# HGRN2 layers' score steps by four blocks, the keys' decay on GpSimd, and two joins between layers reordered

## What is computed

```python
b = jnp.cumsum(lc, axis=-2)                      # lc: log of the forget gate
diff = b[..., :, None, :] - b[..., None, :, :]
decay = jnp.exp(jnp.where(causal[:, :, None], diff, NEG_BIG))
scores = jnp.einsum('bhtk,bhsk,bhtsk->bhts', qc, kc, decay)
o = scores @ vc + jnp.einsum('bhtk,bhkv->bhtv', qc * jnp.exp(b), state)
```

## Time and profile before

| | us |
|---|---|
| median of 3 runs (1487.65 to 1491.38) | 1487.92 |
| the profiled execution | 1488.65 |
| its span | 1486.9 |
| TensorE, matmuls busy | 1444.3 |
| VectorE busy | 960.8 |
| ScalarE busy | 663.6 |
| GpSimd busy | 6.5 |

### The profile page before, as it was taken

How to read it: one execution, slowest core, us unless ns; L and a number is a source line. 1 busy time by engine, 2 the same in 40 slices (tenths; PEclk the granted TensorE clock), 3 DMA queues, 4 the chain that set the end, 5 groups by cost and what they waited for, 6 DMA issues and landing times.

```text
span 1486.9 us, 24212 instructions
## 1 busy us (share of the span) xinstructions
PE 1444.3 (97%) x9165; PEld 1296.3 (87%) x9165; DVE 960.8 (65%) x1755; ACT 663.6 (45%) x1174; POOL 6.5 (0%) x16
## 2 busy tenths in 40 slices
PE   6999999889999999999999998999998999999989
PEld 6888888789998989898999996899887988888878
DVE  6677677654475757575757568567656666776772
ACT  6343333442455555555555646455333424333340
POOL 1000000000000000000000000000000000000000
PEclk9999999999999999999999999999999999999999
DMA  6322212143222222231313131423324222221111
GB/s 197 86 57 78 64 56 62 52 121 94 78 72 71 75 69 85 59 88 55 99 44 100 43 100 29 118 61 94 88 83 113 72 59 85 57 85 56 56 57 57
DMA packets 211721, 114.26 MB, mean 77 GB/s; under 512 B 3742, under 2 KB 209744, under 8 KB 211632
## 3 DMA queue, kind: packets, MB, share of 16 engines
q1 hardware_dynamic: 211200, 112.54, 26.3%
q0 software_dynamic: 432, 0.47, 0.1%
HBM read 110.90 MB, written 2.10 MB: 76 GB/s over the span
## 4 chain that ended last, share of the span: by engine, by line
PE 90%; DVE 5%; issue 3%; ACT 2%; DMA 0%; ACTq 0%; DVEq 0%; SPq 0%
PE ps L545 37%; PE ps L533 35%; PE ps L667 5%; PE ps L813 2%; PE ps L830 2%; PE ps L799 2%; DVE w_lo L1441 1%; PE ps L779 1%; PE ps L696 1%; PE ps L559 1%; PE ps L698 1%; PE ps L685 1%; PE ps L842 0%; DVE op_lo L1480 0%; DMA xt<-in_x 0%
## 5 line engine op out<-in xcount | busy, mean ns | idle before, releaser
L545 PE MATMUL ps<-w_hi,op_hi 128*128 128x256 f32 (+2 forms) x1280 | 418.6, 327 | 17.5 <-DVE op_lo L1485 10.3
L545 PE MATMUL ps<-w_lo,op_hi 128*128 128x256 f32 (+2 forms) x1280 | 404.6, 316 | 0.0
L545 PE MATMUL ps<-w_hi,op_lo 128*128 128x256 f32 (+2 forms) x1280 | 404.4, 316 | 0.0
L533 PE MATMUL ps<-op_hi,w_hi 128*128 128x512 f32 (+1 forms) x800 | 321.6, 402 | 2.2 <-DVE op_lo L1480 2.2
L533 PE MATMUL ps<-op_lo,w_hi 128*128 128x512 f32 (+1 forms) x800 | 307.0, 384 | 0.0
L533 PE MATMUL ps<-op_hi,w_lo 128*128 128x512 f32 (+1 forms) x800 | 305.9, 382 | 0.0
L1441 DVE TENSOR_TENSOR w_lo<-raw,w_hi 128x1024 fp32r<-128x1024 f32 x200 | 242.7, 1226 | 96.2 <-ACT w_hi L1010 96.1
L545 PEld LDWEIGHTS ps<-w_hi,op_hi 128*128 128x128 f32 x1280 | 244.4, 191 | 34.3 <-DVE op_lo L1485 13.2
L545 PEld LDWEIGHTS ps<-w_lo,op_hi 128*128 128x128 f32 x1280 | 244.1, 191 | 5.8
L545 PEld LDWEIGHTS ps<-w_hi,op_lo 128*128 128x128 f32 x1280 | 244.7, 191 | 4.8 <-issue 0.2
L1010 ACT ACTIVATE w_hi<-raw 128x1024 fp32r<-128x1024 f32 x200 | 205.0, 1056 | 43.4 <-PE ps L545 30.5
(11 more groups left out here) (174 smaller groups left out, 1591.2 us busy)
## 6 DMA issues: line engine op xcount, KB each, us to landing
raw<-in_b_w_in SPq DMA_DIRECT2D x80, 512.0 KB, 3.8
raw<-in_a_w_in SPq DMA_DIRECT2D x64, 512.0 KB, 4.2
raw<-in_c_w_in SPq DMA_DIRECT2D x24, 512.0 KB, 4.5
raw<-in_a_w_out SPq DMA_DIRECT2D x16, 512.0 KB, 4.0
raw<-in_b_w_out SPq DMA_DIRECT2D x8, 512.0 KB, 4.0
raw<-in_c_w_out SPq DMA_DIRECT2D x8, 512.0 KB, 4.9
xt<-in_x SPq DMA_DIRECT2D x4, 512.0 KB, 8.2
y<-in_norm_w SPq DMA_DIRECT2D x4, 512.0 KB, 4.6
```

Source lines behind the costliest of these rows:

```text
L533: last = nc.tensor.matmul(bank, a, b, start=(k == 0 and p == 0), stop=(k == KT - 1 and p == 2))
L545: last = nc.tensor.matmul(bank, a, b, start=(k == 0 and p == 0), stop=(k == KT - 1 and p == 2))
```

## The change

Levels are taken two at a time. For m = 2, 8, 32, each group of four blocks is handled by one matmul per tile of 192 columns: 96 queries (blocks 1, 2, 3) moved to the border of the block before, and the same from a second plane `a_far`, where they are moved on by one block (blocks 2, 3) and two (block 3). VectorE makes the second plane (`far_queries`, `farthest_queries`) and copies the three distances out with three masks (`keep_quad`). Level 1 stays the ones-matmul. PSUM banks 2 and 3 become one tensor. The keys' multiplies go to GpSimd, which had no work in the layers. TensorE's steps stand at other `ks`. In VectorE's body `split_products` stands behind `carry`, and the last head's weight splits 4 to 6 at the end. At B's entry the pieces are ordered by halves of the features, and TensorE takes the first four steps of two token tiles before their last four. At C's exit `wide` takes all four tiles in one step, and the weight splits go behind all `split_y`.

The diff at its core (twelve columns of indentation and empty lines taken off; masks, the `h_lo` side of the new order, semaphores and counts left out):

```diff
@@ -40,10 +40,15 @@
 WIDE = 4
 NARROW = ((0, 0), (0, 1), (1, 0), (1, 1), (0, 2), (1, 2), (0, 3), (1, 3))
 OUT_UNITS = WIDE + len(NARROW)
+B_ENTRY = tuple((t, 0) for t in range(4)) + tuple((t, 1) for t in (3, 0, 1, 2))
 FINAL = tuple(WIDE + 1 + NARROW.index((1, t)) for t in range(4))
 C_V_CHUNKS, C_UG_CHUNKS = 8, 16
 LEVELS = 7
-G_STEPS = LEVELS + 1
+QUADS = (2, 8, 32)
+G_STEPS = 2 + len(QUADS)
+KEPT = 2 + 3 * len(QUADS)
+QUAD_MASK = 3 * P // 4 + P // 2 + P // 4
+MASKS = P + P // 2 + QUAD_MASK * len(QUADS)
...
+        def move_keys(n):
+            m = 1 << n
+            nb = S // (2 * m)
+            start = 2 * S - 2 * S // m
+            decay = a_t[:, prev, start:start + 2 * nb].rearrange("p (b u) -> p b u", u=2)[:, :, 1]
+            k = a_k[:, prev].rearrange("p (b u m) -> p b u m", u=2, m=m)[:, :, 0, :]
+            if n:
+                pool.wait_ge(keys_moved, h * LEVELS + n)
+            nc.gpsimd.tensor_tensor(k, k, decay.unsqueeze(2).to_broadcast([P, nb, m]),
+                                    ALU.mult).then_inc(keys_moved, 1)
+        if mix:
+            pool.wait_ge(qk_done, h + 1)
+            move_keys(0)
+            for r in range(len(QUADS)):
+                pool.wait_ge(g_ready, h * G_STEPS + 3 + r)
+                move_keys(2 * r + 1)
+                move_keys(2 * r + 2)
...
+            m = QUADS[r]
+            pe.wait_ge(far_done, h * 6 + 2 * r + 2)
+            pe.wait_ge(keys_moved, h * LEVELS + 2 * r + 1)
+            pe.wait_ge(sd_done, h * KEPT + 2 + 3 * r)
+            for t in range(TT):
+                tile = slice(t * P, (t + 1) * P)
+                of = a_qq[:, prev, :, tile].rearrange("p x (h c) -> p x h c", c=4 * m)[:, :, :, m:]
+                last = nc.tensor.matmul(scores2[:, t * 256:t * 256 + 192], a_k[:, prev, tile], of,
+                                        start=True, stop=True)
+            last.then_inc(g_ready, 1)
         def turn_k():
-            pe.wait_ge(upd, h * LEVELS + LEVELS)
+            pe.wait_ge(keys_moved, h * LEVELS + LEVELS)
             if later:
...
@@ -720,16 +766,19 @@
         steps = {}
         if mix:
-            steps[1] = [turn_v]
-            for g in range(G_STEPS):
-                steps.setdefault(int(2 + 2.4 * g), []).append(lambda g=g: scores(g))
-            steps[21] = [turn_k]
-            steps[23] = [states]
+            for g in range(2):
+                steps[g] = [lambda g=g: scores(g)]
+            steps[1].append(turn_v)
+            steps[4] = [lambda: quad_scores(0)]
+            for r, at in ((1, 10), (2, 16)):
+                steps[at] = [lambda r=r: quad_scores(r)]
+            steps[20] = [turn_k]
+            steps[22] = [states]
             steps[27] = [values]
         if end:
-            steps.setdefault(3, []).append(turn_o)
+            steps.setdefault(4 if mix else 3, []).insert(0, turn_o)
         if mix and not proj:
...
-        for ks in range(B_BANKS * KT):
+        order = list(range(B_BANKS * KT))
+        if static(i) and i == 0:
+            order[4:12] = order[8:12] + order[4:8]
+        for ks in order:
             v, k = divmod(ks, KT)
             if proj:
                 bank = acc[v % 2]
+                if static(i) and i == 0 and ks in (0, 8, 4):
+                    pe.wait_ge(h_lo, 8 * n + {0: 4, 8: 5, 4: 8}[ks])
                 if k == 0:
                     if v in (0, 4, 8, 12, 13):
                         upto = {0: 2, 4: 5, 8: 8, 12: 9, 13: 10}[v]
@@ -986,9 +1040,7 @@
     for g in range(5, HEADS):
         spatial(g)
     for k in range(KT - 1):
-        wide(n, k, (0, 1))
-    for k in range(KT - 1):
-        wide(n, k, (2, 3))
+        wide(n, k, range(TT))
 for t in range(2):
     transpose_x(0, t)
...
+        for t, half in B_ENTRY:
+            h_hi_part(n, t, half)
+def h_hi_part(n, t, half):
+    act.wait_ge(xT_done, 8 * n + 2 * t + half + 1)
+    nc.scalar.activation(h_part(op_hi, n, t, half), turned_part(n, t, half),
+                         ACT.Copy).then_inc(h_hi, 1)
 def h_hi_parts(n, t):
...
@@ -1410,11 +1467,9 @@
         if g >= 1:
             act.wait_ge(cgate_done, g)
         nc.scalar.activation(c_g[:, 0], acc[1][:], ACT.Sigmoid).then_inc(cg_act, 1)
-    for k in range(4):
+    for k in range(KT - 1):
         split_y(n, k)
     split_out(n, (4, 5, 6))
-    for k in range(4, KT - 1):
-        split_y(n, k)
 act.wait_ge(s_set, 1)
...
-            h_lo_parts(n + 1, t)
+    if n + 1 < layers and early:
+        h_lo_parts(n + 1, TT - 1)
+    elif n + 1 < layers:
+        for at, (t, half) in enumerate(B_ENTRY):
+            h_lo_part(n + 1, t, half, at)
...
-                                                score[0][:])
-            else:
-                m = 1 << (g - 1)
-                to = a_sd.rearrange("p t (b u m) -> p (t b) u m", u=2, m=m)[:, :, 1, :]
-                mask = a_mask[:, S + (g - 1) * 256:S + g * 256].rearrange("p (b m) -> p b m", m=m)
-                of = score[g % 2][:, 0:256].rearrange("p (b m) -> p b m", m=m)
-                ins = nc.vector.copy_predicated(to, mask, of)
-            ins.then_inc(sd_done, 1)
+            nc.vector.tensor_tensor(q, q, decay.unsqueeze(2).to_broadcast([P, nb, m]),
+                                    ALU.mult).then_inc(queries_moved, 1)
...
+            dve.wait_ge(sd_done, h * KEPT + count)
+        def far_queries(r):
+            m = QUADS[r]
+            nb = S // (4 * m)
+            start = 2 * S - 2 * S // m
+            decay = a_t[:, prev, start:start + 4 * nb].rearrange("p (b u) -> p b u", u=4)
+            q = a_q[:, prev].rearrange("p (b u m) -> p b u m", u=4, m=m)
+            far = a_far[:, prev].rearrange("p (b u m) -> p b u m", u=4, m=m)
+            moved(2 * r + 1)
+            nc.vector.tensor_tensor(far[:, :, 2:4], q[:, :, 2:4],
+                                    decay[:, :, 1:3].unsqueeze(3).to_broadcast([P, nb, 2, m]),
+                                    ALU.mult).then_inc(far_done, 1)
+        def farthest_queries(r):
+            m = QUADS[r]
+            nb = S // (4 * m)
+            start = 2 * S - 2 * S // m
+            decay = a_t[:, prev, start:start + 4 * nb].rearrange("p (b u) -> p b u", u=4)
+            far = a_far[:, prev].rearrange("p (b u m) -> p b u m", u=4, m=m)
+            dve.wait_ge(far_done, h * 6 + 2 * r + 1)
+            nc.vector.tensor_tensor(far[:, :, 1], far[:, :, 3],
+                                    decay[:, :, 1].unsqueeze(2).to_broadcast([P, nb, m]),
+                                    ALU.mult).then_inc(far_done, 1)
+        def keep_own():
+            mask = a_mask[:, 0:P].unsqueeze(1).to_broadcast([P, TT, P])
+            nc.vector.copy_predicated(a_sd, mask, score[0].rearrange("p (t c) -> p t c", t=TT)).then_inc(sd_done, 1)
+        def keep_pairs():
+            to = a_sd.rearrange("p t (b u) -> p t b u", u=2)[:, :, :, 1]
+            mask = a_mask[:, P:P + 64].unsqueeze(1).to_broadcast([P, TT, 64])
+            nc.vector.copy_predicated(to, mask, score[1][:, 0:256].rearrange("p (t b) -> p t b", t=TT)).then_inc(sd_done, 1)
+        def keep_quad(r, back):
+            m = QUADS[r]
+            nb = P // (4 * m)
+            to = a_sd.rearrange("p t (b c) -> p t b c", c=4 * m)[:, :, :, back * m:]
+            of = scores2[:].rearrange("p (t c) -> p t c", c=256)[:, :, 0:192]
+            of = of.rearrange("p t (x b c) -> p t x b c", x=2, b=nb)
+            of = (of[:, :, 0], of[:, :, 1, :, m:], of[:, :, 1, :, 0:m])[back - 1]
+            at = P + 64 + QUAD_MASK * r + (0, 96, 160)[back - 1]
+            wide = 4 * m - back * m
+            mask = a_mask[:, at:at + nb * wide].rearrange("p (b c) -> p b c", b=nb)
+            nc.vector.copy_predicated(to, mask.unsqueeze(1).to_broadcast([P, TT, nb, wide]),
+                                      of).then_inc(sd_done, 1)
         def carry():
...
             if mix:
-                taken(g)
-                gate() if g == 0 else move_on(g)
-                keep(g)
-            if mix and not proj and g > 1:
-                split_y(n, g - 2)
-            if g == 0 and end:
-                into_y()
-            if mix and not proj and g in (1, 2):
-                split_lo_out(n, g + 1)
-            if mix and not proj and g in (5, 6, 7):
-                split_lo_out(n, g - 1)
-            if proj and g in (1, 2):
-                split_lo_chunk(IN0[n], len(A_PARTS), j, par, g + 1, a_ring)
-            if g == 3 and proj:
-                forget()
-            if g == 6 and proj:
-                query()
-            if g == 7 and proj:
-                products()
-            if g >= 4 and proj:
-                decays({4: (0,), 5: (1, 2), 6: (3, 4), 7: (5, 6)}[g])
-        if mix and not proj:
-            split_y(n, 6)
+                taken(2 + r)
+                kept(2 + 3 * r)
+                move_queries(2 * r + 1)
+                keep_quad(r, 1)
+                moved(2 * r + 2)
+                kept(3 + 3 * r)
+                move_queries(2 * r + 2)
+                keep_quad(r, 2)
```

(31 more changed lines are left out.)

## The result

The changed kernel takes 1466.9 us (median of 4 runs, 1466.3 to 1467.8) where the kernel before takes 1489.3 in the same series: a ratio of 0.985 (95% interval 0.983 to 0.987). The forecast was 1464.5. (The 1487.92 that the forecast started from was the median of the first three of the four runs before.) The profiled execution took 1467.06 us, its span 1465.3, 21.6 less than before.

A forecast was written before the change was run, and what follows sets the result against it. TensorE, busy 97% of the span, was taken as the bound. 19.7 + 1.1 + 1.2 + 4.25 - 3 = 23.3 us off 1488.65 gave 1465.4, or 1464.6 against the median; forecast 1464.5, range 1453 to 1470.

The forecast's parts named there:

- Price of a group: TensorE's score groups: three of 192 columns at 1.37 us replace six at 0.89, saving 19.7 us over 16 heads.
- the term of 1.1 us for one return less in 14 heads: TensorE, turn_o directly before the first group: one 0.08 us return to the projection saved per head, 1.1 us.
- Rival D: TensorE's score passes: holes in the streamed operand halve its rate, 61 us lost, 1526 us; chance 0.03.
- The waits: Steady heads: GpSimd's keys' multiplies disturb VectorE's, 0.2 us in each of 14 heads, 3 us lost; ends 0 and 34.
- the chain's slack: VectorE between two groups: chain of 2.9 us inside a 3.8 us cover, 0.9 spare; cover about 0.4 at the first group.
- Rival B: Disturbance with 0.8 to 1.0 us multiplies, or 0.9 us copies: 0.6 to 1.2 us per head lost, 1470 to 1483; chance 0.20.
- A's band: Whole kernel as forecast, 1453 to 1470 us; chance 0.60.
- Rival C: Exclusion with 1.2 us GpSimd multiplies: TensorE waits before groups 1 and 2, 1500 us; loss from about 1.05; chance 0.09.
- The drains: Last head of each HGRN2 layer: idle stays about 5 us and the clock still falls, gain 0, bounds -2 to +2.
- Attention entry: Attention layer's start: TensorE starts 2.4 us earlier, half kept because of the lower clock, 1.2 us; bounds 0 and 4.2.
- gMLP exit: gMLP layer's output steps: three TensorE gaps of 1.32, 1.47 and 1.46 us vanish, 4.25 us saved; bound below 3.
- The prediction's own signs: Trace checks: 192-column passes starting at 0.16 us, heads about 30.3 us; wrong if passes exceed 0.2 or heads aren't below 31.

The follow-up runs named there:

- 96-column run: Changed kernel with the weight split ahead of into_y, each score pass streaming 96 columns (one plane) instead of 192; 1436.1 us, single execution.
- flat operand: Changed kernel with each score pass streaming 192 side-by-side columns of one plane instead of runs with holes; 1467.1 us, single execution.
- the kernels without waits: Changed kernel with GpSimd on one element (1452.0 us), second and third groups one step later (1454.7), weight split ahead of into_y (1453.9), or the last two together (1454.1).
- the better order: Changed kernel with VectorE's weight split of chunk 2 ahead of into_y instead of behind it; 1453.9 us (ratio 0.976).

## Why the prediction was right, and where its terms were off

The sum was 23.3 us against the profiled execution; 21.6 came. The parts:

- **Price of a group.** Forecast 1.37, measured 1.31 without a wait, 1.40 with one (1.26 + 0.14). Three groups are 4.11 in the changed kernel, as forecast. The forecast took 8 x 0.161 for the stream and 0.08 more for the return. But 1.31 is 8 x 0.163: the stream is right, and there is no return beside it. In the trace the passes of a group start 0.163 apart, the projection matmul only 0.03 behind the last of them, and its slower start makes up for that. In the same way a 64-column group costs 0.90 = 8 x 0.112, and the term of 1.1 us for one return less in 14 heads stood for nothing: turn_o's four transposes take 0.43 up to the group now (107.44 to 107.87) and took 0.35 with 0.09 of return before. The floor under the 64-column passes is shown by the 96-column run; that it is the weight load was argued only. Nor is it shown that streaming sets the 128-column passes: the 14 of the values step cost (1.48 + 0.31 - 0.23) / 14 = 0.111 each, the same as 64 and 96 columns. Rival D is excluded by the flat operand.
- **The waits.** The term that was mis-sized. 3 us were taken for 14 heads, 0.2 each; twelve heads wait and lose 0.8 to 1.0 each, 11.4 us (the kernels without waits are 13 us faster in all). Two things were missed. The text set the chain against the cover for one group at a time, and took VectorE to be ready for the second. But all of VectorE's work between two groups has to fit: behind the first it is 5.5 us (chain, weight split, forget, first gate product), and TensorE's interval is 5.4. So lateness of 0.5 at the first group is carried to the next one instead of ending. That uses up part of the chain's slack (0.9 by the prediction), and the 0.56 of exclusion is then more than what is left. And exclusion reached an instruction outside the chain, the gate product L1638 (mean 750 ns against 426 in the better order). Rival B had the mechanism and a size of 0.6 to 1.2 a head, which is what the steady heads show; the total stayed in A's band because the groups and the ends of the layers gave more than forecast (below), which was luck. The exclusion itself is as the Trainium skill tells it in "SBUF — State Buffer", section "Who interferes with whom": this trace agrees, the engine that starts second takes 0.98 or 0.81 instead of 0.42, and in the better order it is VectorE that starts first at the first group and takes 0.43. The estimate of 0.56 us plus dispatch per multiply (from "GPSIMD Engine Reference") meets 0.71 where two take 1.42 (0.65 and 0.69 with a pause between them), and 0.83 as the mean.
- **Rival C.** Its turning point of 1.05 us wasn't reached; mean 0.83.
- **The drains.** Forecast 0, measured 2.2 and 2.7 for the last heads, of which 1.2 was counted for the groups' price. The idle times came as laid out, 1.54 and 3.98 (forecast 1.5 and 3.5):

```profile
260.69 1.54 PE L713 MATMUL scores<-scratch 128*128 128x192 f32 x8 [1.54 <-DVE scratch L1718]
266.21 2.74 PE L713 MATMUL scores<-scratch 128*128 128x192 f32 x8 [3.98 <-DVE scratch L1707]
```
  What was wrong is the clock. In this row of stretches the granted clock is the third number from the end (0.87):

```profile
262.00:275.00 13.00, 9.02 (x37) 7.61 (x36) 11.67 (x23) 5.82 (x9) 4.49 (x6) 0.87 0.29 82
```
  13 x 0.13 = 1.7 us of clock are given up, where the earlier trace rows had 3.4. The lower level lasted half as long, though the idle time ahead of it was longer. In part this is the luck of the execution: over 264 to 282 the granted clock is 0.91 in the changed kernel and in the runs with the flat operand and with the old gMLP exit, and 0.81 in the run with the old attention entry, though the code up to there is the same or, with the flat operand, takes as long. The last heads of the four take 28.60, 28.34, 28.34 and 29.67, and in the second HGRN2 layer 28.36, 29.28, 28.45 and 29.12. So about 1 us of a last head's gain comes and goes with the clock. What decides it, no run here tells.
- **Attention entry.** Forecast 1.2. The stretch up to the first turn is 1.9 to 2.0 shorter in the profiled changed kernel and 1.6 to 1.7 in two other runs with the same entry; the wait shrank by 2.85 and by 2.5 there, where 2.4 were worked out.
- **gMLP exit.** Forecast 4.25, measured 4.7 by undoing it, 5.2 between the profiled executions. The forecast added up idle times, but TensorE loses more from start to start: the projection matmul ahead of a gap of 1.30, 1.47 and 1.47 comes 1.69, 1.86 and 1.86 before the next one where 0.23 is usual, 4.7 in all, and the first matmul behind each gap takes 0.34 to its successor, 0.3 more in all.

The prediction's own signs say the same. It named TensorE idle ahead of the second and third group as the sign of B or C, and there is such idle time. It wanted a head's period below 31 us, and of the twelve heads three take 30.81 to 30.85 and nine 30.99 to 31.03.

So the total rests in part on errors that cancel. In the stretches given above, against the forecast: the 14 heads with a projection give 9.7 us where 15.4 were counted (14 x 1.1), the two last heads 4.9 where 2.5 were counted (for the groups; nothing for the drain), the attention entry 1.4 for 1.2, the exit and what follows 5.8 for 4.25. These differences, -5.7 + 2.4 + 0.2 + 1.5, are -1.6, and 23.3 - 21.6 is 1.7. The -5.7 is itself a difference of two errors, nearly all of it in the twelve heads that wait. Their waits cost 11.4 us where 2.4 were counted, while a head without waits takes 30.02, which is 1.59 under the earlier trace rows where 1.31 were counted, 3.4 us in twelve heads. Of that 0.28 the groups explain 0.24 (six of 0.90 against three of 1.31 are 1.47, not 1.23), the return that isn't there takes 0.08 away, and 0.12 lies in the ones-matmuls and in the pace of the 96 projection matmuls, 1 ns each, and stays open. With its other terms as they stood and the waits at their true size, the forecast would have been about 1473, in rival B's band.

## What to carry to other kernels

Set all of an engine's work between two hand-overs against the other engine's interval, not only the chain that ends in the hand-over: with the two about equal, lateness isn't made up but eats the slack of the next hand-over, and a disturbance that would have been harmless there is then paid. Here 0.5 us of lateness alone cost nothing, the exclusion with VectorE in time cost nothing, and both together cost 0.4 to 0.5 us at each of two groups. Look first at what an engine does just before it is needed; here one instruction moved into an idle time was worth 13 us, as much as one contraction step more of cover. Work given to GpSimd beside VectorE is priced with the VectorE instructions that it holds back, also those outside the chain, and the engine that starts first isn't the one that pays.

## What the runs showed of the hardware

A multiply of one element takes 0.32 us on GpSimd and one of 256 some 0.65 to 0.71 when it isn't held back, so nearly half is a fixed cost. An fp32 pass of 64, 96 or 128 columns costs TensorE 0.11 us and one of 192 columns 0.163, the next projection matmul's slower start counted in. That matmul's start must be counted: from the first pass to it alone a pass seems to take 0.101 and 0.146. A gap of 0.23 us in TensorE's row ahead of a group costs 0.50 in its period, and each of the exit's gaps of 1.3 to 1.5 costs about 0.3 more than it shows.
